# A two-block transformer kernel: the gated-recurrence mixer of its last stage, rebuilt

## The reference

```python
def step(state, inp):                      # one chunk of tokens, all heads
    qx, kx, lf, vx = inp
    b = jnp.cumsum(lf, axis=2)
    diff = b[:, :, :, None, :] - b[:, :, None, :, :]
    decay = jnp.where(causal, jnp.exp(jnp.where(causal, diff, 0.0)), 0.0)
    att = jnp.einsum('bhtd,bhsd,bhtsd->bhts', qx, kx, decay)
    o = att @ vx + jnp.einsum('bhtd,bhde->bhte', qx * jnp.exp(b), state)
    b_last = b[:, :, -1:, :]
    state = (jnp.exp(b_last[:, :, 0, :])[..., None] * state
             + jnp.einsum('bhsd,bhse->bhde', kx * jnp.exp(b_last - b), vx))
    return state, o
...
o_hg = o_hg * lax.rsqrt(jnp.mean(jnp.square(o_hg), axis=-1, keepdims=True) + RMS_EPS)
o_hg = o_hg * hg_norm_w                                     # per head, 64 wide
mixed = concatenate([o_nsa * silu(nsa_z), o_sb * silu(sb_z), o_hg * silu(hg_z)])
x = layer_norm(ALPHA * x + mixed @ w_out, ln_g, ln_b)
```

## Time and profile before

| | us |
|---|---|
| median of three runs | 1384.18 |
| lowest, highest | 1381.27, 1385.24 |
| profiled execution | 1384.93 |
| its span | 1383.4 |
| TensorE busy (products) | 1218.8 |
| VectorE busy | 557.7 |
| ScalarE busy | 430.6 |
| GpSimd busy | 106.0 |
| mean granted TensorE clock | 0.931 of full |

### The profile page before, as it was taken

One profiled execution on the slowest core, in us unless ns is written; L12 is line 12 of the kernel. 1 busy time (PEld: TensorE's weight loads), 2 busy tenths in 40 slices (PEclk: granted clock), 3 DMA queues, 4 the chain that ended last, 5 costly groups with the idle time before them and its releaser, 6 DMA issues.

```text
span 1383.4 us, 15153 instructions
## 1 busy us (share of the span) xinstructions
PE 1218.8 (88%) x5264; PEld 679.4 (49%) x5264; DVE 557.7 (40%) x1428; ACT 430.6 (31%) x1096; POOL 106.0 (8%) x138
## 2 busy tenths in 40 slices
PE   4879989999889898979999989989998999878654
PEld 1555454555554443334455555555453656545442
DVE  3234323334554311335442431122236532663885
ACT  0133014444451102232243322214343544660122
POOL 0000000000001000000000000000000000461752
PEclk8889989999998999999999989989999899998776
DMA  9321234562003412432111005241111011000001
GB/s 348 104 92 31 94 129 174 184 225 48 0 1 99 69 17 61 89 102 59 52 61 61 1 12 136 62 167 46 46 35 35 23 62 62 1 1 31 1 17 46
DMA packets 60402, 99.71 MB, mean 72 GB/s; under 512 B 12084, under 2 KB 22145, under 8 KB 60328
## 3 DMA queue, kind: packets, MB, share of 16 engines
q1 hardware_dynamic: 54514, 93.58, 22.1%
q10 hardware_dynamic: 5814, 5.18, 1.2%
HBM read 96.60 MB, written 4.08 MB: 73 GB/s over the span
## 4 chain that ended last, share of the span: by engine, by line
PE 74%; DVE 14%; ACT 5%; issue 2%; DMA 2%; ACTq 1%; DVEq 0%; SPq 0%
PE PR L905 32%; PE PT L798 6%; PE OB L935 6%; PE SC L957 6%; PE PR L798 5%; PE OB L798 4%; PE SC L798 4%; PE PT L972 3%; PE PR L860 3%; DVE stage L1735 2%; DMA ring<-in_w_ada 2%; DVE d L1735 1%; DVE tok L1735 1%; DVE ring L1735 1%; PE PR L813 1%
## 5 line engine op out<-in xcount | busy, mean ns | idle before, releaser
L905 PE MATMUL PR<-ring,hT 128*128 128x512 f32 (+1 forms) x784 | 376.4, 594 | 4.4 <-ACT hT L1244 3.5
L905 PEld LDWEIGHTS PR<-ring,hT 128*128 128x128 f32 x784 | 137.2, 198 | 104.8 <-issue 87.5
L1410 ACT ACTIVATE stage<-stage,nmax 128x256 f32<-128x256 f32 (+7 forms) x200 | 103.7, 519 | 268.1 <-DVE nmax L2087 237.8
L935 PEld LDWEIGHTS OB<-arena,pts 128*128 128x128 f32 (+3 forms) x880 | 129.1, 196 | 97.0 <-issue 76.2
L905 PE MATMUL PR<-hT,ring 128*128 128x512 f32 (+1 forms) x304 | 151.0, 622 | 0.0
L1643 POOL TENSOR_TENSOR arena<-arena 128x192 f32<-128x192 f32 (+1 forms) x118 | 78.6, 666 | 827.4 <-PE OB L935 758.0
L935 PE MATMUL OB<-arena,pts 128*128 128x64 f32 (+4 forms) x880 | 127.2, 273 | 9.2 <-ACT pts L1244 9.1
L957 PE MATMUL SC<-arena 64*128 64x256 f32 (+15 forms) x432 | 111.1, 447 | 10.2 <-DVE nmax L2087 10.2
L1244 ACT ACTIVATE pts<-PT 128x256 f32<-128x256 f32 (+7 forms) x200 | 80.7, 404 | 86.0 <-PE PT L972 63.5
L972 PEld LDWEIGHTS PT<-ident,stage 128*128 128x128 f32 (+3 forms) x440 | 58.6, 144 | 96.7 <-issue 69.5
L972 PE MATMUL PT<-ident,stage 128*128 128x128 f32 (+3 forms) x440 | 85.3, 285 | 13.1 <-DVE stage L1743 9.1
(11 more groups left out here) (346 smaller groups left out, 1332.1 us busy)
## 6 DMA issues: line engine op xcount, KB each, us to landing
ring<-in_w_ada SPq DMA_DIRECT2D x12, 2048.0 KB, 8.3
ring<-in_od_w_in SPq DMA_DIRECT2D x8, 2048.0 KB, 17.1
ring<-in_w_in SPq DMA_DIRECT2D x5, 1536.0 KB, 7.0
ring<-in_ev_w_in SPq DMA_DIRECT2D x3, 2048.0 KB, 7.8
ring<-in_w_in SPq DMA_DIRECT2D x3, 2048.0 KB, 9.9
ring<-in_ev_w_out SPq DMA_DIRECT2D x2, 2048.0 KB, 10.1
ring<-in_od_w_out SPq DMA_DIRECT2D x2, 2048.0 KB, 7.9
ring<-in_w_out SPq DMA_DIRECT2D x2, 2048.0 KB, 7.9
```

The costliest lines, as they stand in the source:

```text
L905: mm = pe.matmul(dst, l, r, start=(k == 0), stop=(k == KT - 1))
L935: mm = pe.matmul(ob[:, h * w:h * w + w], pts[0:rows_, v % 2, n * P:n * P + P], vb, start=(n == 0), stop=(n == len(blocks) - 1))
L1410: give(act.activation(pb[:, s % NP, 0:n], zm[:, s % 2, 0:n], ACT.Exp, bias=nmax[:, row, c:c + 1], scale=-1.0, accum_out=rsum[:, row, c:c + ...
```

## The change

1. **Blocks of 32.** HB is 32. Five levels (h = 1 to 16) and the diagonal are formed in four blocks of 32 tokens: 48 products of 32x32 a pair. Level 32 takes four products of 32x32, level 64 two of 64x64. The mask product is 384 columns wide, followed by a sum of 2x96, one of 2x32 and four writes of 32 partitions.
2. **Cross blocks on ScalarE.** The three blocks that need no mask are copied from PSUM to `att` by ScalarE (`cross_blocks`, `gc_s`), after VectorE's mask product (`gm_s`). The refill of the bank pair and the outputs wait for `gc_s`.
3. **Three sets of operands.** The third lies in `hT`, `d3` and the ring. Differences of tile 2 follow tile 1's products on GpSimd without a wait; tile 3's wait for tile 0's outputs. The exponentials of tiles 0 and 1 come behind steps 75 and 82 (before 78 and 84), those of tile 2 at the stage's start, those of tile 3 within tile 2.
4. **Norm of the heads.** ScalarE squares straight from PSUM (`ho_sq`), VectorE scales straight from PSUM, and `hgnorm` is multiplied into the gate in the attention stage.
5. **State update.** Both heads' halves in instructions of 64x3x64.
6. **Norm of an output tile** in steps (`norm_mean`, `norm_variance`, `norm_factor`) that stand between the head pairs; ScalarE does the scaling (`norm_scale`).
7. **Stick-breaking units.** `close_behind` comes before a step's masking instead of after it.

```diff
-HB = 64
+HB = 32
-GW = NLEV * HB
+GW = 6 * HB
-HG_EARLY = (78, 84)
+HG_EARLY = (75, 82)
...
                     if n >= 2:
-                        pe.wait_ge(gm_s, n - 1)
-                    for l in range(NLEV):
-                        for j in range(2):
-                            u = slice(HB * j, HB * j + HB)
-                            for r in range(2):
...
+                        pe.wait_ge(gc_s, n - 1)
+                    halves = [slice(MN * r, MN * r + MN) for r in range(2)]
+                    for l in range(GW // HB):
+                        for b in range(P // HB):
+                            u = slice(HB * b, HB * b + HB)
+                            for r, q in enumerate(halves):
...
+                    for j in range(2):
+                        for r, q in enumerate(halves):
+                            u = slice(64 * j, 64 * j + HB)
+                            pe.matmul(G[u, r, GW:GW + HB], y[5][q, m, u], y[5][q, m, 64 * j + HB:64 * j + 64],
+                                      start=True, stop=True)
+                    for r, q in enumerate(halves):
+                        mm = pe.matmul(G[0:64, r, GW + HB:GW + HB + 64], y[6][q, m, 0:64], y[6][q, m, 64:P],
+                                       start=True, stop=True)
...
                     pe.wait_ge(gs_s, n + 1)
+                    pe.wait_ge(gc_s, n + 1)
...
+            def cross_blocks(c, m):
+
+                n = c * HP + m
+                G, w = GB[n % 2], att[n % 2]
+                act.wait_ge(gm_s, n + 1)
+                for j in range(2):
+                    u = slice(64 * j, 64 * j + HB)
+                    link(copy(w[u, :, 64 * j + HB:64 * j + 64], G[u, :, GW:GW + HB]))
+                give(copy(w[0:64, :, 64:P], G[0:64, :, GW + HB:GW + HB + 64]), gc_s, n + 1)
...
+                cross_blocks(c, 0)
+                if c >= 2:
+                    norm_sum(c - 2)
+                cross_blocks(c, 1)
...
+                if c >= 2:
+                    norm_square(c - 2)
+                if c == 2:
+                    exponentials(3)
+                cross_blocks(c, 2)
+                if c >= 2:
+                    norm_factor()
+                act.wait_ge(ho_done, HP * (c + 1))
+                give(act.activation(d2[:, 0:384], OB[c % 2][:, 0:384], ACT.Square), ho_sq, c + 1)
+                rsqrt(HGH)
+                if c >= 2:
+                    norm_scale(c - 2)
...
-                if c >= 2:
-                    pool.wait_ge(g_done, HP * (c - 1))
-                    pool.wait_ge(ho_done, HP * (c - 1))
+                if c >= 3:
+                    pool.wait_ge(g_done, HP * (c - 2))
+                    pool.wait_ge(ho_done, HP * (c - 2))
...
+                    stick_end = r_ > 1 and v_units[v - 2][3][0][0] == "sb"
+                    if stick_end:
+                        close_behind(v - 1)
...
-                    if r_:
+                    if r_ and not stick_end:
                         close_behind(v - 1)
...
+            def level_sums(n):
+                G, w = GB[n % 2], att[n % 2]
+                dve.wait_ge(g_done, n + 1)
+                if n >= 2:
+                    dve.wait_ge(ho_done, n - 1)
+                give(tt(gm, G[:, :, 0:GW], bass.AP(levels.tensor, levels.offset, [list(levels.ap[0]), [0, 2], [1, GW]]),
+                        ALU.mult), gm_s, n + 1)
+                link(tt(gm[:, :, 0:3 * HB], gm[:, :, 0:3 * HB], gm[:, :, 3 * HB:6 * HB], ALU.add))
+                link(tt(gm[:, :, 0:HB], gm[:, :, 0:HB], gm[:, :, HB:2 * HB], ALU.add))
+                for b in range(P // HB):
+                    u = slice(HB * b, HB * b + HB)
+                    ins = tt(w[u, :, u], gm[u, :, 0:HB], gm[u, :, 2 * HB:3 * HB], ALU.add)
+                    if b < P // HB - 1:
+                        link(ins)
+                give(ins, gs_s, n + 1)
```

186 lines of the change are left out of this document (96 added, 90 removed).

## The result

The changed kernel takes 1379.19 us as the median of nine runs (1374.76 to 1382.81), against 1385.24 of nine runs of the kernel before (1381.27 to 1389.91). The ratio is 0.9949, with a 95% interval of 0.9928 to 0.9970: faster by 0.5%, where 1.2% was forecast, and 0.2 us outside the range. The profiled execution took 1375.87 us (its span is 1374.1), 9.1 less than the one before; 1368.9 was forecast for it, so 7.0 us are missing there.

The account below looks back on a forecast made before the run. VectorE was taken to bound the mixer's stage, with TensorE waiting at a falling clock. From 1384.93 us, 16.5 gained in the stage and 0.5 lost at the attention's end gave 1368.9; range 1360 to 1379.

Parts of the forecast that it names:

- Attention's end: Attention before the mixer: 3.3 us lost to earlier exponentials, 1 to GpSimd, 3.8 regained; net +0.5, between -4.8 and +4.3.
- the 4.82 goes ... so 3.8 comes back: TensorE's 4.82 us wait at 1243.44 disappears; the copy of the transposed tile is late next, so 3.8 is regained.
- TensorE's pair: Level products of one head pair on TensorE, 108 pieces: 0.95 us, or 1.4 at the low clock.
- Rivals 1: Small TensorE pieces cost what they cost now: 1.7 and 3.4 us a head pair, whole 1381; chance 0.09.
- rival 2: Small TensorE pieces take a fixed 31.6 ns: 3.4 us a pair, 1390; 25 ns would end near 1387; chance 0.05.
- Tile 0: First mixer tile: 22.25 becomes 22.7 us, early output products at the low clock, ScalarE's copy of their operand 0.4 later.
- Tile 1: Second mixer tile: 30.15 becomes 25.0 us, with heads' norm 5.4, two held pairs and some 2 us waiting for TensorE.
- Tile 2: Third mixer tile: 22.0 becomes 24.6 us; TensorE waits some 6 us for GpSimd's products before the next tile.
- Tile 3: Fourth mixer tile: 31.9 becomes 18.5 us, 1.0 of it held by GpSimd's output work; under 20 was the sign.
- Tail: Mixer's end after the last tile: 18.7 becomes 17.7 us, as 0.8 of scaling leaves VectorE.
- A head pair on VectorE: In the mixer, one pair takes VectorE 2.35 us against 3.33, or about 4.1 held by GpSimd against 4.6 to 4.9.
- Rival 3: New waits keep TensorE at 1.2 GHz: 22.3 us a mixer tile plus 3 to 4 of waits, 1379; chance 0.11.

Follow-up runs that it names:

- early_back: Changed kernel with the exponentials of tiles 0 and 1 behind steps 78 and 84 again; 1374.7 us, ratio 0.9920 to the kernel before.
- both_back: Changed kernel with those exponentials behind steps 78 and 84 and the group's output gated behind the masking again; 1374.6 us, ratio 0.9925 to the kernel before.
- exp3_sooner: Changed kernel with tile 3's exponentials at the end of tile 1 on ScalarE instead of within tile 2; 1375.8 us, ratio 0.9927 to the kernel before.
- early_exp3: Changed kernel with tiles 0 and 1's exponentials behind steps 78 and 84, tile 3's at the end of tile 1; 1365.9 us, ratio 0.9849 to the kernel before.

## Why the prediction was wrong

The mechanism was right: VectorE leaves the command, GpSimd's products for tile 3 take it, and tiles 1 and 3 shrink. Sizes were off, and one term of the attention's end was wrong in kind. First the shares by stretch, then the prices.

- **Attention's end, "+0.5": wrong, +3.8.** The loss was priced rightly, 3.3 for the exponentials between two units (the row shows 3.20). The step that failed is "the 4.82 goes ... so 3.8 comes back". The transposes near 1243 did start at once, 1240.98. The fifth of them then waited 3.61 for a bank that VectorE frees with a residual, which stands behind a scan chain held by GpSimd. Gating the group earlier brought 0.5 at most, not 3.8 (early_back and both_back). I had named the copy as what is late next; it was the bank. The bound on this side, +4.3, held for the profiled run, but not for the four traces with A at 79, +6.4: it left out that the clock was at 0.50 behind the idle stretch, for 3 us in two traces of six and for 16 in four, 2.5 us dearer.
- **TensorE's pair, "0.95 and 1.4": 1.28 and 1.69,** and one pause of 1.7 to 1.8 us in each of the first two tiles. The price of a piece followed neither columns nor the old 15.4 ns. Rivals 1 and 2 were wrong as priced for a single pair; rival 2's fixed time, 29 ns, exists, but only in a run of instructions twice as long as the kernel's. Against it I had put only the 15.4 ns of a burst. The 1387 worked out beside rival 2 takes off nothing for waits, where rival 2's own 1390 takes off 5; on the same footing it would be 1382.
- **Tile 0, 22.7: 24.1.** The step on ScalarE's copy, "0.4 later", was 0.9: the first early product starts 8.56 us into the tile (1270.04) for 7.6 before. The rest went with the clock, 0.79 there; at 0.85 the same code took 22.1 (early_back).
- **Tile 1, 25.0: 23.3.** The heads' norm was sized at 5.4 and took 3.95, from ScalarE's square at 1303.52 to the end of the gate at 1307.47, and one pair was held where I had two. The step after it, "waits some 2 us for TensorE", was 2.70 (at 1302.06).
- **Tile 2, 24.6: 25.5.** The right gate: TensorE waits 8.05 for GpSimd, where some 6 were named. exp3_sooner and early_exp3 show that this wait is what the tile's end hung on; in S the better place was worth 3.7 and 5.6.
- **Tile 3, 18.5: 20.4,** over the 20 that was named as a sign. The wrong term is "1.0 held by GpSimd's output work": it was 2.0 and 2.1 at two places, as each hold lasts up to one GpSimd instruction of 2.4 us.
- **Tail, 17.7: 19.4.** The last twelve output products took 7.90 for 7.01 before, at a granted clock of 0.68 for 0.76 in their windows, and VectorE waits for them; the scaling that left VectorE was not on that path.
- **A head pair on VectorE, 2.35 unheld, about 4.1 held: 2.2 and 4.6.** The sizes stand, but the conclusion that blocks of 32 pay was never tested in the ledger, which moved all parts at once. Two pairs of profiles give them 0 in S within 1 us. The saved microsecond lies in pairs that GpSimd stretches or that wait for TensorE, and TensorE's pauses take the rest.
- The state update went as priced, four instructions of 0.35, and the products with `hgnorm` cost 0.4 at most.

Rival 3 gave 1379, and 1379.19 was measured, but that is chance. Its ground was a clock that the new waits keep low; the clocks of the five stretches were 0.79, 0.78, 0.73, 0.83 and 0.68 for 0.85, 0.79, 0.81, 0.66 and 0.68 before, no lower as a whole.

The rest between 1375.87 and the median of 1379.19 isn't in the ledger. The clock at step 75 can explain 2.5 of it in part of the runs; that was read in other kernels' traces, and not shown for the nine runs.

## What to carry to other kernels

When a change bundles a relief and a removed dependency, price each alone and both together: here 3.1 and 3.7 us apart and 16.0 joined, once the exponentials stood where they should, and one part of the bundle, the blocks of 32, was worth nothing that the runs could show. Put long work of a side engine where its queue is idle and nobody takes turns with it; two moves of a few lines (tiles 0 and 1's exponentials back behind TensorE's own work, tile 3's to the end of tile 1) brought 13 us by the medians, twice what the change itself did. Where GpSimd and VectorE share a stage, look which of VectorE's operations on the path could take a PSUM operand: those kept their time here. Cutting GpSimd's instructions short made each hold shorter, but not the kernel. And before a difference of 1 or 2 us between two traces is given to an edit, look for a pause or another clock that only one of them has.

## What the hardware showed unexpectedly

- Long rows of small products run out of instructions: 256 in 3.73 us when sustained, against 216 in 1.28 us in a burst, with pauses of 1.0 to 1.9 us marked as issue in the trace.
- After one and the same idle stretch of 3.20 us TensorE ran at half the clock in six traces of six, at once or within 0.2 us. In two it was at full clock again some 3 us later, in four only after 16 (0.80 and 0.51 to 0.52 over 17 us), 2.5 us apart in A.
- VectorE's operations between SBUF operands end shortly after the GpSimd instruction that they meet (0.35 us became 1.17 and 2.01); with a PSUM operand they keep their time (0.34).
- 60 pieces 64 wide and 108 pieces 32 wide took TensorE about 1.0 and 1.28 us: by the sizes of the products the small blocks have half the multiplications, and the pair got dearer.
